# Turned weights copied ahead of the exponentials, short weights scaled on ScalarE, mean sums moved up, and a first key unit gated by quarters

## The reference, cut to what matters

```python
def even_mixer(hl, hc, ...):                       # convolution group and attention group
    a = conv_module(...)                           # 31 taps, then LayerNorm over 512 channels, then silu
    att_l = window_attn_latent(q, k, v, kc, vc, sink)
    att_c = attn_context(qc, kc, vc, sink)         # latent queries see 512 keys, context queries 256
    y = concat([a, att]) @ w_out

p = softmax(concat([scores * scale, sink]))        # exponentials, divided by their sum
o = p @ v

def odd_mixer(hl, hc, ...):
    g = h @ w_in[:, 4 * ML_DIM:] + b_gate          # 16 gate rows
    k = h @ w_in[:, ML_DIM:2 * ML_DIM]             # keys, head by head
```

## Time and profile before

| what | value |
|---|---|
| time of three runs, us | 1789.6, 1792.38, 1792.55 (median 1792.38) |
| time of the profiled execution, us | 1785.82 |
| its span, first to last instruction, us | 1784.0 |
| mean granted clock of TensorE | 0.994 |
| PE busy, us (share) | 1731.0 (97%) |
| DVE, ACT, POOL busy, us | 1126.3, 605.1, 76.5 |

### The profile page before, as it was taken

The page is one execution under the profiler, slowest core; times in us unless marked ns, Lnnn a source line. Parts: engine busy times, 40 slices in busy tenths (PEclk is TensorE's granted clock), DMA queues, the critical chain, the costliest instruction groups (busy, mean ns, idle before and its releaser), DMA issues.

```text
span 1784.0 us, 23465 instructions
## 1 busy us (share of the span) xinstructions
PE 1731.0 (97%) x9273; PEld 1456.3 (82%) x9273; DVE 1126.3 (63%) x1745; ACT 605.1 (34%) x809; POOL 76.5 (4%) x141
## 2 busy tenths in 40 slices
PE   8999999999988999999999999999999999899998
PEld 5888888878636788888887888888878999899997
DVE  5577667876984667766787577333345446765455
ACT  5322132333455432212223322132233333544443
POOL 0001000000100000100100000000000000000000
PEclk9999999999999999999999999999999999999999
DMA  9465556532212245555554453322222222245543
GB/s 388 173 192 174 190 171 190 168 133 95 80 48 90 92 150 197 177 172 180 187 180 147 142 193 113 118 95 94 74 93 96 71 72 95 95 147 175 196 164 121
DMA packets 51744, 255.57 MB, mean 143 GB/s; under 512 B 6224, under 2 KB 9808, under 8 KB 35280
## 3 DMA queue, kind: packets, MB, share of 16 engines
q1 hardware_dynamic: 33088, 186.31, 30.6%
q0 software_dynamic: 18576, 68.17, 12.1%
HBM read 251.25 MB, written 1.05 MB: 141 GB/s over the span
## 4 chain that ended last, share of the span: by engine, by line
PE 89%; DVE 6%; ACT 2%; DMA 1%; issue 1%; SPq 0%; DVEq 0%; ACTq 0%
PE ps L557 28%; PE ps L558 28%; PE ps L559 28%; DVE w_lo L1462 1%; DVE y L1692 1%; PE ps L985 1%; ACT w_hi L1117 1%; PE ps L1014 1%; DMA mod_raw<-in_mod_first 1%; PE ps L800 0%; PE ps L812 0%; PE ps L587 0%; PE ps L616 0%; PE ps L826 0%; DVE t_ring L1533 0%
## 5 line engine op out<-in xcount | busy, mean ns | idle before, releaser
L557 PE MATMUL ps<-hn_hi,w_hi 128*128 128x512 f32 (+1 forms) x1768 | 637.4, 361 | 5.6 <-DVE hn_lo L1540 4.0
L558 PE MATMUL ps<-hn_lo,w_hi 128*128 128x512 f32 (+1 forms) x1768 | 631.7, 357 | 0.0
L559 PE MATMUL ps<-hn_hi,w_lo 128*128 128x512 f32 (+1 forms) x1768 | 631.6, 357 | 0.0
L1462 DVE TENSOR_TENSOR w_lo<-raw,w_hi 128x2048 fp32r<-128x2048 f32 (+2 forms) x179 | 365.9, 2044 | 334.9 <-ACT w_hi L1117 334.7
L1117 ACT ACTIVATE w_hi<-raw 128x2048 fp32r<-128x2048 f32 (+2 forms) x179 | 307.0, 1715 | 714.6 <-PE ps L559 706.9
L557 PEld LDWEIGHTS ps<-hn_hi,w_hi 128*128 128x128 f32 x1768 | 334.3, 189 | 61.4 <-issue 7.0
L559 PEld LDWEIGHTS ps<-hn_hi,w_lo 128*128 128x128 f32 x1768 | 334.1, 189 | 49.0
L558 PEld LDWEIGHTS ps<-hn_lo,w_hi 128*128 128x128 f32 x1768 | 334.2, 189 | 47.1
L557 PE MATMUL ps<-a_hi,w_hi 128*128 128x512 f32 (+1 forms) x704 | 255.5, 363 | 2.0 <-DVE a_lo L1607 1.7
L558 PE MATMUL ps<-a_lo,w_hi 128*128 128x512 f32 (+1 forms) x704 | 255.2, 362 | 0.0
L559 PE MATMUL ps<-a_hi,w_lo 128*128 128x512 f32 (+1 forms) x704 | 255.2, 362 | 0.0
(11 more groups left out here) (229 smaller groups left out, 1205.2 us busy)
## 6 DMA issues: line engine op xcount, KB each, us to landing
raw<-in_w_up SPq DMA_DIRECT2D x88, 1024.0 KB, 4.9
mod_raw<-in_mod_w POOLq DMA_DIRECT2D x128, 512.0 KB, 3.9
raw<-in_w_downA SPq DMA_DIRECT2D x32, 768.0 KB, 4.3
raw<-in_w_downB SPq DMA_DIRECT2D x32, 640.0 KB, 3.9
raw<-in_w_od_in SPq DMA_DIRECT2D x16, 1024.0 KB, 4.9
mod_raw<-in_mod_first SPq DMA_DIRECT2D x8, 1024.0 KB, 11.0
raw<-in_w_ev_in SPq DMA_DIRECT2D x7, 1024.0 KB, 5.0
raw<-in_w_ev_out SPq DMA_DIRECT2D x4, 1024.0 KB, 5.1
```

The source lines that it names most:

```text
L557: pe.matmul(o, lh, rh, start=first, stop=False)
L558: pe.matmul(o, lh, rl, start=False, stop=False)
L559: return pe.matmul(o, ll, rh, start=False, stop=last)
L1462: dve.tensor_tensor(w_lo[:, u0 % 2, 0:n], raw[:, u0 % 2, 0:n], w_hi[:, u0 % 2, 0:n], ALU.subtract).then_inc(lo_made, 1)
```

## The change

It has seven parts.

1. ACT copies the turned weights of j - 2 before the exponentials of j, and no longer after them.
2. The weights of short steps are scaled on ACT, behind the exponentials of the next long step, and no longer on DVE. `p_made` becomes two semaphores.
3. The sums for the mean are cut into four and stand in PE's steps 14 and 15 ahead of the turning.
4. The last value product (group 7) goes to bank 4, and does not wait for the low part of group 6.
5. ACT's squares are spread over three loop steps, between the last head copies.
6. 40 taps instead of 48 come before the loop, the rest over 12 steps and not 10; the two passes for the low parts of the first output units move from loop steps 12 and 13 to 6 and 11.
7. In the odd mixer the first three key tiles follow their own gate tile at once, then two gate tiles follow each other; keys 4 and 5 wait for the third quarter of the low part alone.

```diff
+        def value_bank(g):
+            return 4 if g == 7 else 0
-        AHEAD_OF_LOOP = 48
+        AHEAD_OF_LOOP = 40
...
-                pe.wait_ge(p_made, j + 1)
+                pe.wait_ge(p_made[s], j // 2 + 1)
...
+                for c in {NJ - 2: (0, 1), NJ - 1: (2, 3)}.get(j, ()):
+                    mean_sum(c)
                 if 2 <= j < NJ + 1:
                     turn(j - 1)
...
-                if j == NJ - 1:
-                    mean_sums()
...
+            for k in range(KT):
+                gate_part(k)
+                if k < 3:
+                    first_keys(k)
+                elif k > 3:
+                    first_keys(k - 1)
...
+            def normalise(j):
+                tt, s, qt = ATT[j]
+                act.wait_ge(den_made, j + 1)
+                for h2 in range(2):
+                    p = weight_place(s)[:, h2, :]
+                    last = act.activation(p, p, ACT.Copy, scale=att_cols[:, 5, 2 * j + h2:2 * j + h2 + 1])
+                last.then_inc(p_made[1], 1)
...
+                if 2 <= j < NJ + 2:
+                    turned(j - 2)
                 if j < NJ:
                     expo(j)
                 if j == NJ:
                     act.preload_act_table(ACT.Sqrt)
-                if 2 <= j < NJ + 2:
-                    turned(j - 2)
...
+                if j < NJ + 1 and ATT[j - 1][1] == 1:
+                    normalise(j - 1)
                 if j >= 6 and (j - 6) % 4 < 2 and j < NJ + 4:
                     att_head(2 * ((j - 6) // 4) + (j - 6) % 4)
...
-                    normalise(j - 1)
+                    if ATT[j - 1][1] == 0:
+                        normalise(j - 1)
...
-                if j in (12, 13):
-                    rest_of(E + 7 + j - 12)
+                if j in (6, 11):
+                    rest_of(E + 7 + (j == 11))
```

More of the change, by code:

```diff
@@ L231, in build @@
         den_made = sem("den_made")
-        p_made = sem("p_made")
+        p_made = [sem("p_made0"), sem("p_made1")]
         pT_mm = sem("pT_mm")
@@ L373, in taps_by @@
         def taps_by(j):
-            return min(TAPS, AHEAD_OF_LOOP + (TAPS - AHEAD_OF_LOOP) * (j - 1) // 10)
+            return min(TAPS, AHEAD_OF_LOOP + (TAPS - AHEAD_OF_LOOP) * (j - 1) // 12)
         ATT = [(tt, s, qt) for tt in range(4) for qt in range(2) for s in range(2)]
@@ L816, in values @@
             def values(tt, s):
+                at = value_bank(2 * tt + s)
                 g = 2 * tt + s
                 pe.wait_ge(pT_made, 4 * tt + 2 + s + 1)
-                if g >= 1:
+                if g == 7:
+                    pass
+                elif g >= 1:
                     pe.wait_ge(mix_made, g)
@@ L825, in values @@
                     for h2 in range(2):
-                        last = pe.matmul(ps[64 * h2:64 * h2 + 64, 0, 0:LAT], v_att[:, kt, 64 * h2:64 * h2 + 64],
+                        last = pe.matmul(ps[64 * h2:64 * h2 + 64, at, 0:LAT], v_att[:, kt, 64 * h2:64 * h2 + 64],
                                          turned_place(s)[:, h2, i, :], start=(i == 0), stop=(kt == 3))
@@ L844, in conv_part, with mean_sum @@
                     last.then_inc(conv_mm, 1)
[L846 to L851, removed]
+            def mean_sum(c):
+                if c == 0:
+                    pe.wait_ge(conv_made, 2)
+                    pe.wait_ge(tap_done, TAPS)
+                last = pe.matmul(ps[:, CONV_BANK, :], ones, y[:, c, :], start=(c == 0), stop=(c == CT - 1))
+                if c == CT - 1:
+                    last.then_inc(ln_mm, 1)
             NJ = len(ATT)
@@ L935, in _ @@
             begin(u)
[L936 to L961, removed]
@@ new lines, in gate_part, with first_keys @@
+            def gate_part(k):
+                pe.wait_ge(hn_made, KT * 4 + k + 1)
+                last = three(ps[0:16, bank(u), :], weights(u, k * 16, (k + 1) * 16),
+                             (hn_hi[:, k, :], hn_lo[:, k, :]), k == 0, k == KT - 1)
+                if k == KT - 1:
+                    last.then_inc(unit_mm, 1)
+            def first_keys(k):
+                if k == 0:
+                    pe.wait_ge(late_lo, late_done(4, 1))
+                    pe.wait_ge(unit_evac, u)
+                if k == KT // 2:
+                    pe.wait_ge(late_lo, late_done(4, 2))
+                if k == 6:
+                    pe.wait_ge(lo_made, u + 2)
+                for i in range(4):
+                    last = three(ps[:, KEY_BANKS[i], 0:DH],
+                                 (hn_hi[:, k, i * P:(i + 1) * P], hn_lo[:, k, i * P:(i + 1) * P]),
+                                 weights(u + 1, k * DH, (k + 1) * DH), k == 0, k == KT - 1)
+                return last
@@ new lines, in _ @@
+            for k in range(KT):
[4 more added lines that the diff above has]
+                    first_keys(k - 1)
+            pe.wait_ge(gate_rows, 1)
+            for i in range(4):
+                turned = pe.transpose(ps[:, bank(u), i * 16:(i + 1) * 16],
+                                      gact[0:16, 0, i * P:(i + 1) * P], ident[0:16, 0:16])
+            turned.then_inc(gates_mm, 1)
+            last = first_keys(KT - 1)
@@ L1308, in att_head @@
                 act.wait_ge(pv_mm, g + 1)
-                act.activation(hn_hi[:, CT + g // 2, tokens(g % 2)], ps[:, 0, 0:LAT], ACT.Copy).then_inc(att_hi, 1)
+                act.activation(hn_hi[:, CT + g // 2, tokens(g % 2)], ps[:, value_bank(g), 0:LAT], ACT.Copy).then_inc(att_hi, 1)
             expo(0)
@@ L1320, in _ @@
                     act.preload_act_table(ACT.Sqrt)
-                if 2 <= j < NJ + 2:
-                    turned(j - 2)
[L1323 to L1328, removed]
+                if j < NJ + 1 and ATT[j - 1][1] == 1:
+                    normalise(j - 1)
                 if j >= 6 and (j - 6) % 4 < 2 and j < NJ + 4:
                     att_head(2 * ((j - 6) // 4) + (j - 6) % 4)
+                for c in {NJ + 1: (0, 1), NJ + 2: (2,), NJ + 3: (3,)}.get(j, ()):
+                    act.wait_ge(ln_cent, c + 1)
+                    if c == 3:
+                        act.wait_ge(ln_added, 1)
+                    act.activation(acc if c == 0 else sq[:, c % 2, :], y[:, c, :], ACT.Square).then_inc(ln_sq, 1)
             act.wait_ge(ln_mm, 2)
@@ L1760, in normalise @@
                     last = dve.tensor_scalar(p, p, att_cols[:, 5, 2 * j + h2:2 * j + h2 + 1], None, ALU.mult)
-                last.then_inc(p_made, 1)
+                last.then_inc(p_made[0], 1)
             def ln_add(c):
@@ L1795, in _ @@
                     dve.wait_ge(att_hi, g + 1)
-                    dve.tensor_tensor(hn_lo[:, CT + g // 2, tokens(g % 2)], ps[:, 0, 0:LAT],
+                    dve.tensor_tensor(hn_lo[:, CT + g // 2, tokens(g % 2)], ps[:, value_bank(g), 0:LAT],
                                       hn_hi[:, CT + g // 2, tokens(g % 2)], ALU.subtract).then_inc(mix_made, 1)
```

## The result

The median of 12 runs went from 1788.68 us (1785.31 to 1792.55) to 1792.83 us (1792.24 to 1795.79). The ratio is 1.0029, 95% interval [1.0020, 1.0038]: slower by 0.2 to 0.4%; the two medians alone give 1.0023. The profiled execution took 1792.68 us with a span of 1790.9, 6.9 more than before, at a mean granted clock of 0.990.

A forecast was written before the change was run, and what follows sets the result against it. The round between ACT and PE bounds the loop; 0.45 + 5.29 - 3.03 - 1.3 - 0.7 = +0.7, plus clock falls 1.74 and 2.6, about +5.0 us: 1790.8 profiled, 1797.4 on the median, 0.28% slower. Range 1790 to 1802.

The forecast's parts named there:

- the rival of a clock that holds: Attention loop: its gaps bring no fall of the clock, no change, +0.7 to +2.4 us; chance 0.27.
- Scaling pair 0.89: Loop, ACT: the two scalings of short weights take 0.89 us, bounds 0.76 and 1.02.
- Start +0.45: Loop start: the copy of step 0 comes ahead of the exponentials of step 2, +0.45 us.
- Six pairs 54.34 at full clock, +5.29: Loop, exponentials of step 2 to step 14: longer ACT-PE rounds take 54.34 us against 49.05, +5.29.
- Two falls in the loop, 2.6: Loop: PE idles 2.2 us four times; two falls of the clock taken, 1.3 each, +2.6 us.
- End 14.26 at full clock, one fall of 1.74: Exponentials of step 14 to first output unit: 14.26 us against 17.29, -3.03; a clock fall adds 1.74.
- First output unit -1.3: First output unit's 24 matmuls, 6.80 us before, take 1.3 less at full clock.
- Odd mixer -0.7: Odd mixer: first keys fill PE's wait of 1.41 before the second gate tile; some 0.7 given back, -0.7 us.
- Taps and low parts at nothing: Loop, DVE: taps gained for eight scalings lost are covered by the longer round, no cost.
- Up to 5 us: Loop, DVE: cost of the taps without the longer round's cover, up to 5 us.
- 1.98 a long product: Loop: a copy waiting for a long product ahead of the exponentials adds 1.88 and 0.10 back to the round.
- DVE as the pace: Loop: DVE sets the pace and the change frees it, -8.3 us, 1784.1 on the median; chance 0.13.

The follow-up runs named there:

- e5: Changed kernel with PE multiplying constants nobody reads in its idle time ahead of the short turnings; ratio to before 1.0007.
- e4: Kernel before with part 7 alone, the first three key tiles behind their own gate tile; ratio to before 1.0009.
- e9: Changed kernel with part 6 alone undone (48 taps ahead of the loop, low parts in steps 12 and 13); ratio to before 1.0035.
- e2: Changed kernel with part 2 undone, short weights scaled on DVE again, copies still ahead; ratio to before 0.9981.
- e3: Changed kernel with parts 1 and 2 both undone; ratio to before 0.9976.
- e12: e11 with part 7 and products of constants in two waits of the odd mixer; ratio to before 0.9933, 1776.90 us.
- e7: Kernel before with part 1 alone, the copy ahead of the next long exponentials; ratio to before 0.9998.
- e11: Kernel before with parts 1, 3 and 4, and a head's low part made on DVE ahead of denominator and scaling; ratio to before 0.9940, 1778.20 us.
- e8: Kernel before with part 2 alone, short weights scaled on ACT behind the copy; ratio to before 1.0027.
- e1: Changed kernel with part 1 undone, exponentials ahead of the copy again; ratio to before 0.9991.

## Why the prediction was right, point by point

It said 0.28% slower; the ratio says 0.29%. That the two agree so well is in part luck. The time forecast for the median, 1797.4 us, was 4.6 too high: it started from three runs of before with a median of 1792.38, and twelve runs have 1788.68. The measured 1792.83 lies beside the 1793.1 that the rival of a clock that holds would have given from the same start, so the time by itself does not tell the two apart; the ratio and the profile do. The mechanism is the one that was forecast. The terms, one by one:

- **Scaling pair 0.89:** 0.89 (489.84).
- **Start +0.45:** the exponentials of step 2 stand at 488.04 instead of 487.40, and PE's scores ahead of them were already 0.19 late; 0.45 remain.
- **Six pairs 54.34 at full clock, +5.29:** e5, where the clock holds, has 53.83, and none of its six pairs is more than 0.16 off the forecast. With falls they took 58.22, over the 54 to 57 that the prediction named.
- **Two falls in the loop, 2.6:** mis-sized. Three came, and the pairs they hit took 1.42, 1.23 and 1.47 more than forecast: 4.1 us. The price was right, the count too low by one.
- **End 14.26 at full clock, one fall of 1.74:** 15.74 with its fall (from the timeline; 15.81 by the chain above) and 14.20 in e5 without it, so the fall cost 1.54 there.
- **First output unit -1.3:** 5.67 (562.07 to 567.74) against 6.80, -1.1.
- **Odd mixer -0.7:** -0.76, in the changed kernel and in e4; the wait that was left of it is 0.46 at the fifth tile.
- **Taps and low parts at nothing, covered by the longer round:** e9 bears it out; e2 and e3 show the price without that cover, waits of 4.42 and 2.39 us in one pair, where before has 1.02. "Up to 5 us" holds as a bound.

At the turned gate rows of the odd mixer the changed kernel is 6.42 us behind (1360.15 against 1353.73), where the forecast had 5.0; the third fall in the loop is most of the difference. At the end the profiled spans differ by 6.9. Behind that place the changed kernel's profile has falls at 1468 (1.7) and 1553 (3.4) where before has 1358 (1.7) and 1549 (1.7). e4 and e12 show that such falls come and go where the program is the same.

**What the prediction had not seen** is who carries the loss. It costed parts 1 and 2 together, and charged 1.98 a long product to the copy's place. e7 shows that this place alone costs nothing, and e11 that it can shorten the pairs: without the scaling on ACT, the copy and the exponentials leave a round of 5.47, and the product's wait has room. e8 shows that the scaling alone costs as much as the whole change. Both prices hold only in company. With 1.5 taken off for each fall (an estimate, from the 9.06 of e8 against the 7.58 of e1) the pairs go from 49.05 to 51.2 with part 2 alone (e8, three falls), to 48.0 with part 1 alone (e7, one fall), and to 53.8 with both (e5): +2.2 and -1.0 make +4.8 together.

**The rivals of the prediction.** DVE as the pace fell: part 2 takes 0.62 us a pair off DVE, and alone makes the kernel slower by 0.27% (e8). But the prediction read one round of the loop, and passed over a later stretch of the chain before, from 525.19 to 536.42, in which DVE is on it nearly all the time, with the scaling of a short step (L1760), two low parts of weights (L1462) and the step for which the exponentials of step 14 wait:

```profile
527.00 0.62 DVE sq L1760 x2
...
527.95 2.20 DVE w_lo L1462
...
532.79 2.20 DVE w_lo L1462
...
536.25 0.17 DVE att_cols L1745
```

There DVE did set the pace. Even so the move of the scaling did not pay there: with part 2 alone (e8) the last two pairs take 10.13 and 8.27 us, before 10.14 and 8.33.

The Trainium skill, Perfetto Trace Analysis, section Optimizing Scalar/DVE Operations, says that offloading work to Scalar may make sense if DVE is saturated; here it did not, and the trace shows why: PE waits 15.9 us for ACT's scaling, while in the round that the prediction read before, nobody waited for DVE's. The clock that holds was forced in e5, at the end of the loop too: 1.0007, within the +0.7 to +2.4 us that it was given (1.2 us by the ratio).

What stays open is which gap brings a fall: of PE's gaps of 2.60, 2.06, 2.13 and 2.06 us three did and one did not (499.78), while e1 had two of 2.12 without one and e8 two of 2.12 with one each. Nor does the same place do the same each time: the wait of 1.77 from which the prediction took its measure brought a fall before and none in the changed kernel, where it stands at 1363.96.

## What to carry to other kernels

Before moving work from the busiest engine to another, look in the chain for who is in the round: 0.89 us a pair put on ACT, for which PE waited, cost more than 0.62 a pair brought in on DVE, for which nobody waited in that round. And read the chain over the whole loop, since its last pairs hung on DVE and not on that round. Where a slower round opens gaps on PE, add falls of the clock to the bill (1.2 to 1.5 us each here, about as much again as the round), and test the two apart by filling the gaps with products that nobody reads. Take a bundle of edits apart: here the change was 0.29% slower, and two of its seven parts alone are 0.44% faster than before.

## What was not expected of the hardware

Every fall between 490 and 566 us, in all these profiles, took 1.7 us of clock or twice that, whether the gap of PE ahead of it was 1.90 (e9, at 492.11) or 4.42 us (e2). And the clock can fall while PE still idles: in e2 it was 0.80 from 506 to 507 and 0.50 from 507 on, with PE's next work at 509.13.
